# Six norms of a one-core block kernel: the sum of squares over the first three quarters moves from TensorE to VectorE

## The chip, the cores and the metric

The kernel runs on one core of one Trainium2 chip, in one launch. Five engines work from their own instruction streams and meet at semaphores: TensorE (PE, with its weight loads as PEld), VectorE (DVE), ScalarE (ACT), GpSimd (POOL, here only an issuer of DMAs) and SyncE (SP, also an issuer of DMAs). The metric is the device time of one launch in microseconds (us), as the median of several runs.

## The reference

A 256-token sequence of width 1024 in float32 passes one first block (Fourier mixing and a bidirectional gated delta rule, then a gated convolutional feed-forward net) and two hybrid layers (retention, gated linear recurrence and forgetting attention, merged, then an MLP). What matters here is that each of these six sublayers ends in a root-mean-square norm of its output before the residual addition:

```
def rms_norm(x, g):
    xf = x.astype(jnp.float32)
    y = xf * lax.rsqrt(jnp.mean(xf * xf, axis=-1, keepdims=True) + EPS)
    return (y * g.astype(jnp.float32)).astype(x.dtype)
...
    x = x + gt_m * rms_norm(merged @ w_out, g_post_mix)
    h = rms_norm(x, g_pre_mlp) * (1.0 + sc_f) + sh_f
    f = jnp.square(jax.nn.relu(h @ w1)) @ w2
    return x + gt_f * rms_norm(f, g_post_mlp)
```

The mean runs over the 1024 features of each token.

## The kernel before

**Layout.** Activations lie feature-major: 128 features on the partitions, eight feature blocks, 256 tokens along the free axis. A mean over features is therefore a sum over eight blocks and over the 128 partitions. TensorE does both at once: a 128x128 matrix `omean`, filled with 1/1024, is multiplied with each block of squares, and the eight products accumulate in PSUM bank 7, where every partition then holds the mean.

**The stream of chunks.** All weights come in 233 chunks of 1 MB, in the order of their use, into four slots `raw`, loaded by SP as soon as the chunk four places earlier is done. Each chunk is split in two parts for a three-product scheme: ScalarE writes `w_hi` (L1108), VectorE writes `w_lo` = raw - w_hi (L1651), into two slots each. TensorE then runs 48 products a chunk (16 weight tiles, three products each, L397 to L399), after a wait on `lo_ready`, and counts `chunk_done`. ScalarE may start on chunk n + 2 when chunk n is done. Queues are in program order on every engine; the order is written out by hand.

**The six norms.** They stand behind the output projection of the first block (`N_OUT1`, four chunks), its down-projection (`N_DOWN`, eleven chunks), and in each of two layers behind the output projection (`L_WOUT`, four chunks) and the second half of the MLP's down-projection (eight chunks, `deep_chunk`). Their outputs stay in four PSUM banks. When a bank (a quarter of the features) is complete, ScalarE squares it into SBUF (`square`, L1149, 128x512) and counts `norm_sq`. TensorE runs `norm_part` (L497 to L503) for that quarter: two products of plain float32, 128x256. For quarter q it stands one output bank behind: in the output projections the parts of quarters 0, 1 and 2 follow the chunks 1, 2 and 3, and in the two kinds of down-projection they follow the first product group of the next bank. The part of quarter 3 stands at the end. The last product counts `norm_ms`; ScalarE takes the root (`root`, L1154), VectorE the reciprocal (L1698), and the residual follows. Behind the norm, TensorE's queue goes on with products of a conditioning projection (`ada_mm`, L517), whose weights POOL loads when the buffers' last products are done.

The other seven norms (`norm`, L505) take their squares from SBUF, all four parts in a row, and are not touched.

Of the kernel before, what the change touches and what calls it, by code (L numbers as in the profile page):

```python
# [19 lines left out]
T = 256  # L20
# [70 lines left out]
def build_program(nc, io, layers=LAYERS):  # L91
# [6 lines left out]
    with ctx:  # L98
# [294 lines left out]
        def _(pe):  # L393
# [103 lines left out]
            def norm_part(k, sq, q):  # L497
# [4 lines left out]
                if q == 3:  # L502
                    last.then_inc(S("norm_ms"), 1)  # L503

            def norm(k, sq):  # L505
                for q in range(4):
                    norm_part(k, sq, q)
# [59 lines left out]
            for c in range(4):  # L567
                n = N_KV + c
                begin(n, n)
                bank = KV_BANK[c]  # L570
                feat_chunk(n % 2, bank + 1, 1)
                if c == 0:
                    pe.wait_ge(S("sw_wide"), 1)
                    pe.wait_ge(S("mod_lo"), 16)
                    small_mm(xc, 0)
                    small_mm(norm_h1, T).then_inc(S("ab_rows_mm"), 1)
                if c == 1:
                    pe.wait_ge(S("ab_rows"), 1)
                    small_tr(ab_rows, 4, 16).then_inc(S("ab_mm"), 1)
                feat_chunk(n % 2, bank, 0).then_inc(S("chunk_done"), 1)  # L580
# [286 lines left out]
            for c in range(4):  # L867
                begin(N_OUT1 + c, None)
                (turned_chunk if c == 0 else feat_chunk)((N_OUT1 + c) % 2, c, 1).then_inc(S("chunk_done"), 1)
                if c > 0:  # L870
                    norm_part(2, norm_sq1, c - 1)
            norm_part(2, norm_sq1, 3)
            ada_mm(14)
# [20 lines left out]
            for at_, (o, k, n, b) in enumerate(down):  # L894
                first_of_chunk, last_of_chunk = at_ % 16 == 0, at_ % 16 == 15
                if at_ == 34:
                    ada_tr(2)
                if first_of_chunk:
                    pe.wait_ge(S("lo_ready"), n + 1)
                if at_ == 0:  # L900
                    pe.wait_ge(S("evicted"), J_UP + 19)
                if o == 2 and k == 0:
                    pe.wait_ge(S("evicted"), J_DOWN)
                if o == 0 and k >= 16:
                    pe.wait_ge(S("mid_ready"), k + 1)
                last = mm3(ps[:, 2 + o // 2, o % 2 * T:o % 2 * T + T], w_hi[:, n % 2, b * P:(b + 1) * P], w_lo[:, n % 2, b * P:(b + 1) * P],
                           mid_hi1[:, k, :], mid_lo1[:, k, :], k == 0 and o % 2 == 0, k == FB - 1, shared=True)
                if last_of_chunk:
                    last.then_inc(S("chunk_done"), 1)
                elif o % 2 == 1 and k == FB - 1:  # L910
                    last.then_inc(S("down_done"), 1)
                if o % 2 == 0 and o >= 2 and k == FB - 1:
                    norm_part(4, sq_down, o // 2 - 1)
            norm_part(4, sq_down, 3)
            pe.wait_ge(S("ada_out"), 3)
# [3 lines left out]
            for L in range(layers):  # L919
# [129 lines left out]
                for c in range(4):  # L1049
                    n, j = n0 + L_WOUT + c, j0 + JL(L_WOUT) + c  # L1050
                    begin(n, j if c < 2 else None)
                    if c == 0:
                        out_chunk(n % 2, c, 0, 4 * L + 1).then_inc(S("chunk_done"), 1)
                    else:
                        feat_chunk(n % 2, c, 0).then_inc(S("chunk_done"), 1)
                        norm_part(ns + 1, a6, c - 1)
                norm_part(ns + 1, a6, 3)
                ada_mm(22 if L == 0 else 30)
# [6 lines left out]
                for hf in range(2):  # L1065
# [13 lines left out]
                    for c in range(8):  # L1079
                        begin(n + 8 + c, None)  # L1080
                        deep_chunk((n + 8 + c) % 2, c, hf, ready=all_ready if c == 0 else None).then_inc(S("chunk_done"), 1)
                        if hf == 1 and c % 2 == 0 and c >= 2:
                            norm_part(ns + 3, a6, c // 2 - 1)
                norm_part(ns + 3, a6, 3)
                if L == 0:
# [7 lines left out]
        def _(act):  # L1093
# [129 lines left out]
            for c in range(4):  # L1223
                n = N_KV + c
                prep(n + 2, (n + 2) % RAW, n % 2)
                if c == 0:
                    act.wait_ge(S("ab_rows_mm"), 1)
                    act_(ab_rows[:, :], ps[:, 7, :], ACT.Copy).then_inc(S("ab_rows"), 1)
                if c == 2:
# [412 lines left out]
        def _(dve):  # L1642
# [52 lines left out]
            def root_done(k):  # L1695
# [3 lines left out]
                dve.wait_ge(S("norm_rstd"), k + 1)  # L1699

            def pipe(m, pre, lo):

# [126 lines left out]
            def decay_part():  # L1829

                dve.wait_ge(S("ab_act"), 1)
                order(ts(sm[:, 2, :], sm[:, 2, :], 0.5, 0.5, ALU.mult, ALU.add))
# [194 lines left out]
            order(tt(gs[:, 0, :], mod[:, 16:24], V("g_post_mix", KT), ALU.mult))  # L2027
            job(N_OUT1, 3)
            dve.wait_ge(S("ada_out"), 1)
# [96 lines left out]

            job(N_DOWN, 9)
            layer_vectors(0)
# [3 lines left out]
            for L in range(layers):  # L2132
# [248 lines left out]
                for c in range(4):  # L2381
# [6 lines left out]
                    if c == 3:  # L2388
                        wout_lo(3)
                        prep(n + 2, (n + 2) % RAW, n % 2)  # L2390
                job(n0 + L_WOUT, 3)
                residual(ns + 1, 2 + 2 * L, 0, a5, gs[:, 0, :])
                prep(n0 + L_MLP + 1, (n0 + L_MLP + 1) % RAW, (n0 + L_MLP + 1) % 2)
                modulate(ns + 2, 4 + 2 * L, x, a5, gs[:, 1, :], mod[:, 24:32], act_hi[1], act_lo[1])
                for hf in range(2):
# [18 lines left out]
                    if hf == 1:  # L2414
                        mods_out()
                    job(n + 8, 8 if hf == 0 else 6)
                if L + 1 < layers:
# [144 lines left out]
```

## Time and profile before

| | us |
|---|---|
| median of 3 runs | 1755.04 (1750.12 to 1759.26) |
| the profiled execution | 1759.32 |
| its span, first to last instruction | 1757.5 |
| PE busy | 1664.9 (95%) |
| DVE busy | 1099.0 (63%) |
| ACT busy | 815.0 (46%) |

The span is 1.8 us shorter than the execution's own time. Busy times are unions over an engine's instructions; matmuls overlap each other in the pipeline, so that a matmul row's duration (280 ns) is longer than its distance to the next (114 to 118 ns). A product of plain float32 shows in the trace as two matmul instructions, so a part of a norm, two products, is a row of x4.

### The profile page before, as it was taken

What the parts mean: (1) busy time and instruction counts of PE and PEld (TensorE: products, weight loads), DVE (VectorE), ACT (ScalarE), POOL (GpSimd) and SP (SyncE); (2) the same over time, 40 slices, a digit from 0 to 9 for tenths busy, and PEclk for the clock granted to TensorE, in tenths of its full rate; (3) what the DMA queues carried; (4) which work ended last, traced back from release to release, by engine and by line L of the source; (5) the groups of instructions that cost most, each with busy time, mean ns of one, the idle gap of its engine ahead of it and who ended that gap; (6) DMA issues with size and microseconds to landing.
All of it is one profiled execution on the core that took longest, in us unless ns stands there. A gap on an engine that the chain in (4) does not pass through costs nothing.

```text
span 1757.5 us, 34379 instructions
## 1 busy us (share of the span) xinstructions
PE 1664.9 (95%) x15242; PEld 1586.6 (90%) x15242; DVE 1099.0 (63%) x1382; ACT 815.0 (46%) x1057; POOL 34.0 (2%) x68
## 2 busy tenths in 40 slices
PE   5997999999998999999998999989999999989997
PEld 4996888799996999999997999979999999979996
DVE  4576744689946455678866545455546878565463
ACT  3346324433434436458544434445454675444352
POOL 0001000000000000000001000000000000000000
PEclk8999999999999999999999999999999999999998
DMA  9336344744556446445559655555454555725551
GB/s 395 147 125 259 147 164 168 270 168 167 174 185 250 147 161 197 147 167 175 184 192 350 223 181 183 189 193 183 154 173 159 176 179 186 278 99 192 192 191 72
DMA packets 45529, 331.40 MB, mean 189 GB/s; under 512 B 5072, under 2 KB 5072, under 8 KB 5456
## 3 DMA queue, kind: packets, MB, share of 16 engines
q1 hardware_dynamic: 36032, 260.73, 42.9%
q0 software_dynamic: 9216, 67.11, 9.7%
q8 instruction: 113, 1.85, 0.4%
q10 hardware_dynamic: 144, 1.51, 0.2%
q14 instruction: 24, 0.20, 0.0%
HBM read 326.18 MB, written 1.05 MB: 186 GB/s over the span
## 4 chain that ended last, share of the span: by engine, by line
PE 80%; DVE 7%; ACT 5%; DMA 5%; issue 1%; SPq 1%; POOL 0%; ACTq 0%; DVEq 0%; POOLq 0%
PE ps L397 21%; PE ps L399 21%; PE ps L398 21%; PE ps L450 4%; DVE w_lo L1651 3%; ACT w_hi L1108 2%; PE ps L517 2%; DMA raw<-stream 2%; PE ps L501 2%; DMA ada_alt<-ada 1%; PE ps L674 1%; PE ps L685 1%; DMA ada_raw<-ada 1%; DMA ada_f<-ada 1%; PE ps L1002 1%
## 5 line engine op out<-in xcount | busy, mean ns | idle before, releaser
L397 PE MATMUL ps<-act_hi,w_hi 128*128 128x256 f32 x2672 | 757.6, 284 | 17.3 <-DVE act_lo L1720 4.6
L1651 DVE TENSOR_TENSOR w_lo<-raw,w_hi 128x2048 fp32r<-128x2048 f32 x207 | 474.4, 2292 | 467.9 <-ACT w_hi L1108 467.5
L398 PE MATMUL ps<-act_lo,w_hi 128*128 128x256 f32 x2672 | 747.9, 280 | 0.0
L399 PE MATMUL ps<-act_hi,w_lo 128*128 128x256 f32 x2672 | 747.8, 280 | 0.0
L1108 ACT ACTIVATE w_hi<-raw 128x2048 fp32r<-128x2048 f32 (+1 forms) x229 | 421.7, 1842 | 525.0 <-PE ps L399 506.1
L397 PEld LDWEIGHTS ps<-act_hi,w_hi 128*128 128x128 f32 x2672 | 507.3, 190 | 24.3 <-issue 13.3
L398 PEld LDWEIGHTS ps<-act_lo,w_hi 128*128 128x128 f32 x2672 | 506.8, 190 | 0.8
L399 PEld LDWEIGHTS ps<-act_hi,w_lo 128*128 128x128 f32 x2672 | 506.7, 190 | 0.0
L397 PE MATMUL ps<-mlp_hi,w_hi 128*128 128x256 f32 x512 | 143.9, 281 | 0.1
L398 PE MATMUL ps<-mlp_lo,w_hi 128*128 128x256 f32 x512 | 142.5, 278 | 0.0
L399 PE MATMUL ps<-mlp_hi,w_lo 128*128 128x256 f32 x512 | 142.5, 278 | 0.0
L398 PEld LDWEIGHTS ps<-mlp_lo,w_hi 128*128 128x128 f32 x512 | 96.8, 189 | 0.2
L397 PEld LDWEIGHTS ps<-mlp_hi,w_hi 128*128 128x128 f32 x512 | 96.3, 188 | 0.5 <-DVE w_lo L1659 0.3
L399 PEld LDWEIGHTS ps<-mlp_hi,w_lo 128*128 128x128 f32 x512 | 96.3, 188 | 0.0
L2076 DVE SCALAR_TENSOR_TENSOR gacc<-gpad,vectors,gacc 128x256 f32<-128x256 f32 x176 | 84.5, 480 | 15.6 <-ACT gacc L1379 10.3
L450 PE MATMUL ps<-h_up,raw 128*128 128x256 f32 x352 | 81.2, 381 | 0.7
L450 PEld LDWEIGHTS ps<-h_up,raw 128*128 128x128 f32 x352 | 64.7, 190 | 11.3 <-ACT h_up L1369 3.1
L397 PE MATMUL ps<-w_hi,act_hi 128*128 128x256 f32 x256 | 72.5, 283 | 0.0
L399 PE MATMUL ps<-w_hi,act_lo 128*128 128x256 f32 x256 | 71.6, 280 | 0.0
L398 PE MATMUL ps<-w_lo,act_hi 128*128 128x256 f32 x256 | 71.4, 279 | 0.0
L397 PE MATMUL ps<-mid_hi,w_hi 128*128 128x256 f32 x176 | 50.7, 288 | 3.7 <-DVE w_lo L1651 2.6
L1612 ACT ACTIVATE mlp_hi<-rsq 128x512 fp32r<-128x512 f32 x32 | 20.2, 632 | 72.6 <-DVE rsq L2403 72.6
(420 smaller groups left out, 2008.1 us busy)
## 6 DMA issues: line engine op xcount, KB each, us to landing
raw<-stream SPq DMA_DIRECT2D x233, 1024.0 KB, 4.9
ada_raw<-ada POOLq DMA_DIRECT2D x46, 1024.0 KB, 6.6
ada_alt<-ada POOLq DMA_DIRECT2D x12, 1024.0 KB, 12.1
ada_f<-ada POOLq DMA_DIRECT2D x6, 1024.0 KB, 8.7
ada_f<-ada SPq DMA_DIRECT2D x4, 1024.0 KB, 13.9
ada_a<-ada SPq DMA_DIRECT2D x3, 1024.0 KB, 20.0
s<-s SPq DMA_DIRECT2D x4, 512.0 KB, 10.1
consts_stage<-consts_a SPq DMA_DIRECT2D x1, 1728.0 KB, 32.7
```

Of the source, the lines that this page charges most:

```text
L397: mm(out, ah, bh, start=first, stop=False, skip_group_check=shared)
L398: mm(out, ah, bl, start=False, stop=False, skip_group_check=shared)
L399: return mm(out, al, bh, start=False, stop=last, skip_group_check=shared)
L450: mm(ps[:, bank, 0:T], raw[:, slot, k * P:(k + 1) * P], h_up[:, k, :], start=k == 0, stop=k == KT - 1)
L501: last = mm(ps[:, 7, 0:T], omean, sq[:, b, :], start=b == 0, stop=b == KT - 1)
L517: last = mm(ps[strip:strip + 32, bank, c * T:(c + 1) * T], cs_wide[:, k, 32 - 3 * j:64 - 3 * j], ada_home(i, c)[:, k * T:(k + 1) * T], sta ...
L674: last = mm(ps[r:r + 64, INV_BANK[q], j * 64:(j + 1) * 64], B01[d][r:r + 64, t0 + j // 4, j % 4, r:r + 64], Tm[r:r + 64, q, j, :], start=T ...
L685: last = mm(ps[r:r + 64, INV_BANK[q], j * 32:(j + 1) * 32], Uc[r:r + 64, q, j, :], half(X[r:r + 64, q, j, :], d, 1 << lvl), start=True, st ...
L1108: act_(w_hi[:, s2, o:CH], raw[:, s4, o:CH], ACT.Copy).then_inc(S("hi_ready"), 1)
L1612: act_(mlp_hi[:, bass.ds((i + c) * 2, 2), :], rsq[:, s, :].rearrange("p (b t) -> p b t", b=2), ACT.Copy)\
L1651: tt(w_lo[:, s2, :], raw[:, s4, :], w_hi[:, s2, :].bitcast(f32), ALU.subtract).then_inc(S("lo_ready"), 1)
L2076: ins = stt(acc, src, w, acc, ALU.mult, ALU.add)
```

## The change

The products between the chunks are gone from the six norms. VectorE adds quarter 1 of the squares onto quarter 0 (128x512), later quarter 2 onto the result, and then folds the two blocks of the result into one (128x256), counting a new semaphore `norm_pre`. TensorE runs three products behind the last chunk: the folded block once `norm_pre` has come, and the two blocks of quarter 3 once their squares have come. A second edit frees one semaphore for this: the ScalarE copy that counted `ab_rows` now counts `ab_act`, and VectorE's later wait on `ab_act` asks for 2 in place of 1.

```diff
+            def norm_folded(i, k, sq):
+
+                pe.wait_ge(S("norm_pre"), i + 1)
+                mm(ps[:, 7, 0:T], omean, sq[:, 0, :], start=True, stop=False)
+                pe.wait_ge(S("norm_sq"), 4 * k + 4)
+                mm(ps[:, 7, 0:T], omean, sq[:, 6, :], start=False, stop=False)
+                mm(ps[:, 7, 0:T], omean, sq[:, 7, :], start=False, stop=True).then_inc(S("norm_ms"), 1)
...
-                    pe.wait_ge(S("ab_rows"), 1)
+                    pe.wait_ge(S("ab_act"), 1)
...
                 (turned_chunk if c == 0 else feat_chunk)((N_OUT1 + c) % 2, c, 1).then_inc(S("chunk_done"), 1)
-                if c > 0:
-                    norm_part(2, norm_sq1, c - 1)
-            norm_part(2, norm_sq1, 3)
+            norm_folded(0, 2, norm_sq1)
...
-                if o % 2 == 0 and o >= 2 and k == FB - 1:
-                    norm_part(4, sq_down, o // 2 - 1)
-            norm_part(4, sq_down, 3)
+            norm_folded(1, 4, sq_down)
...
                         feat_chunk(n % 2, c, 0).then_inc(S("chunk_done"), 1)
-                        norm_part(ns + 1, a6, c - 1)
-                norm_part(ns + 1, a6, 3)
+                norm_folded(2 + 2 * L, ns + 1, a6)
...
-                        if hf == 1 and c % 2 == 0 and c >= 2:
-                            norm_part(ns + 3, a6, c // 2 - 1)
-                norm_part(ns + 3, a6, 3)
+                norm_folded(3 + 2 * L, ns + 3, a6)
...
+            def square_sum(k, sq, q):
+
+                dve.wait_ge(S("norm_sq"), 4 * k + q + 1)
+                order(tt(sq[:, 0:2, :], sq[:, 0:2, :], sq[:, 2 * q:2 * q + 2, :], ALU.add))
+                if q == 2:
+                    tt(sq[:, 0, :], sq[:, 0, :], sq[:, 1, :], ALU.add).then_inc(S("norm_pre"), 1)
...
-                dve.wait_ge(S("ab_act"), 1)
+                dve.wait_ge(S("ab_act"), 2)
...
-            job(N_OUT1, 3)
+            job(N_OUT1, 2)
+            square_sum(2, norm_sq1, 1)
+            job(N_OUT1 + 2, 1)
+            square_sum(2, norm_sq1, 2)
...
-            job(N_DOWN, 9)
+            job(N_DOWN, 7)
+            square_sum(4, sq_down, 1)
+            job(N_DOWN + 7, 2)
+            square_sum(4, sq_down, 2)
...
-                job(n0 + L_WOUT, 3)
+                job(n0 + L_WOUT, 2)
+                square_sum(ns + 1, a6, 1)
+                job(n0 + L_WOUT + 2, 1)
+                square_sum(ns + 1, a6, 2)
...
-                    job(n + 8, 8 if hf == 0 else 6)
+                    if hf == 0:
+                        job(n + 8, 8)
+                    else:
+                        job(n + 8, 4)
+                        square_sum(ns + 3, a6, 1)
+                        job(n + 12, 2)
+                        square_sum(ns + 3, a6, 2)
```

(`order(...)` marks an instruction and has VectorE wait for its end; `job` on VectorE writes the `w_lo` of so many chunks.)

How the queues change is seen at three places. The first is TensorE's queue before, at the boundary of chunks 1 and 2 of the first block's output projection (act_hi_54, act_lo_56 are the split activations, norm_sq_116 the squares, consts_common holds `omean`):

```order
L397 MATMUL ps<-act_hi_54,w_hi 128x256
L398 MATMUL ps<-act_lo_56,w_hi 128x256
L399 MATMUL ps<-act_hi_54,w_lo 128x256
L501 MATMUL ps<-norm_sq_116,consts_common 128x256 [waits norm_sq]
L501 MATMUL ps<-norm_sq_116,consts_common 128x256
L397 MATMUL ps<-act_hi_54,w_hi 128x256 [waits lo_ready]
L398 MATMUL ps<-act_lo_56,w_hi 128x256
```

Now the chunks follow each other without a break there. The second place is the end of that projection, in TensorE's queue with the change (L508 takes the folded block, L510 and L511 the fourth quarter, L525 is `ada_mm`):

```order
L397 MATMUL ps<-act_hi_54,w_hi 128x256
L398 MATMUL ps<-act_lo_56,w_hi 128x256
L399 MATMUL ps<-act_hi_54,w_lo 128x256
L508 MATMUL ps<-norm_sq_116,consts_common 128x256 [waits norm_pre]
L510 MATMUL ps<-norm_sq_116,consts_common 128x256 [waits norm_sq]
L511 MATMUL ps<-norm_sq_116,consts_common 128x256
L525 MATMUL ps<-ada_raw,silu_c_wide 32x256 [waits ada_loaded0]
```

Before, four L501 stood in the place of L508 to L511, with one wait ahead of each pair. The third place is VectorE's queue with the change, in the same projection (L1652 is the `w_lo` split, L1705 and L1707 are the new additions, L1699 the reciprocal of the root):

```order
L1652 TENSOR_TENSOR w_lo<-raw,w_hi 128x2048 [waits hi_ready]
L1705 TENSOR_TENSOR norm_sq_116<-norm_sq_116 128x512 [waits norm_sq]
L1652 TENSOR_TENSOR w_lo<-raw,w_hi 128x2048 [waits hi_ready,dve_order]
L1705 TENSOR_TENSOR norm_sq_116<-norm_sq_116 128x512 [waits norm_sq]
L1707 TENSOR_TENSOR norm_sq_116<-norm_sq_116 128x256 [waits dve_order]
L2041 TENSOR_TENSOR mod<-mod_raw,vectors 128x24 [waits ada_out]
L2043 SCALAR_TENSOR_TENSOR gain_scale<-mod,vectors 128x8 [waits mods_done]
L2044 TENSOR_TENSOR gain_scale<-mod,vectors 128x8 [waits dve_order]
L1699 RECIPROCAL rstd<-std 128x256 [waits norm_std,dve_order]
```

Before, the splits stood there back to back. One addition now stands between the last two splits, and the other two stand behind the last.

## Rows read from the trace of the kernel before

**Rows 1.** The page: busy times of the engines; shares of the chain by line.

```profile
PE 1664.9 (95%) x15242; PEld 1586.6 (90%) x15242; DVE 1099.0 (63%) x1382; ACT 815.0 (46%) x1057; POOL 34.0 (2%) x68
PE ps L397 21%; PE ps L399 21%; PE ps L398 21%; PE ps L450 4%; DVE w_lo L1651 3%; ACT w_hi L1108 2%; PE ps L517 2%; DMA raw<-stream 2%; PE ps L501 2%; DMA ada_alt<-ada 1%; PE ps L674 1%; PE ps L685 1%; DMA ada_raw<-ada 1%; DMA ada_f<-ada 1%; PE ps L1002 1%
```

**Rows 2.** The chain in order of time, layer 0's output projection: start, us, what.

```profile
947.11 1.82 PE ps L501 x8
948.93 3.63 PE ps L517 x64
952.85 11.37 DMA ada_alt<-ada
```

**Rows 3.** Timeline of PE, first block's output projection and last MLP: start, us, instruction, xcount.

```profile
308.19 0.28 PE L399 MATMUL ps<-act_hi,w_lo 128*128 128x256 f32 x1
308.31 1.02 PE L501 MATMUL ps<-norm_sq,consts_common 128*128 128x256 f32 x4
...
309.29 0.28 PE L398 MATMUL ps<-act_lo,w_hi 128*128 128x256 f32 x1
...
314.70 0.28 PE L399 MATMUL ps<-act_hi,w_lo 128*128 128x256 f32 x1
...
315.80 0.28 PE L398 MATMUL ps<-act_lo,w_hi 128*128 128x256 f32 x1
...
321.04 0.28 PE L399 MATMUL ps<-act_hi,w_lo 128*128 128x256 f32 x1
...
1736.81 0.28 PE L399 MATMUL ps<-mlp_hi,w_lo 128*128 128x256 f32 x1
1736.92 1.02 PE L501 MATMUL ps<-s,consts_common 128*128 128x256 f32 x4
...
1737.90 0.28 PE L398 MATMUL ps<-mlp_lo,w_hi 128*128 128x256 f32 x1
```

**Rows 4.** Stretches: us; PE, PEld, DVE, ACT, POOL busy (x); granted clock; DMA; GB/s.

```profile
504.00:508.00 4.00, 4.00 (x38) 4.00 (x37) 2.29 (x1) 1.94 (x2) 0.00 (x0) 1.00 0.79 262
928.00:932.00 4.00, 4.00 (x36) 4.00 (x36) 1.61 (x2) 2.40 (x2) 0.00 (x0) 1.00 1.01 426
936.00:940.00 4.00, 4.00 (x38) 4.00 (x37) 2.29 (x1) 0.96 (x2) 0.00 (x0) 1.00 1.01 426
1124.00:1128.00 4.00, 4.00 (x36) 4.00 (x35) 0.11 (x1) 1.61 (x1) 0.00 (x0) 1.00 0.23 39
1134.00:1138.00 4.00, 4.00 (x38) 4.00 (x37) 2.28 (x1) 0.00 (x0) 0.00 (x0) 1.00 0.50 209
1704.00:1708.00 4.00, 4.00 (x38) 4.00 (x37) 2.29 (x1) 0.28 (x1) 0.00 (x0) 1.00 0.57 233
```

**Rows 5.** Timeline of DVE, end of the first block's output projection.

```profile
317.03 2.29 DVE L1651 TENSOR_TENSOR w_lo<-raw,w_hi 128x2048 fp32r<-128x2048 f32 x1 [4.22 <-ACT w_hi L1108]
319.24 0.18 DVE L2030 TENSOR_TENSOR mod<-mod_raw,vectors 128x24 f32<-128x24 f32 x1
```

**Rows 6.** DVE additions of like form: all of L2356 (min/median/max ns), one L2038.

```profile
L2356 DVE TENSOR_TENSOR s<-s,s x8: 691/693/694, 910.6 to 1520.3; 128x512 f32<-128x512 f32 x8
...
338.10 0.42 DVE L2038 TENSOR_TENSOR act_lo<-h_up,act_hi 128x256 fp32r<-128x256 f32 x1 [0.23 <-ACT act_hi L1371]
```

**Rows 7.** Timeline of ACT, three squares and two roots, first block and layer 0's MLP.

```profile
316.90 0.58 ACT L1149 ACTIVATE norm_sq<-ps 128x512 f32<-128x512 f32 x1
...
321.35 0.60 ACT L1149 ACTIVATE norm_sq<-ps 128x512 f32<-128x512 f32 x1 [3.78 <-PE ps L399]
323.17 0.47 ACT L1154 ACTIVATE std<-ps,eps 128x256 f32<-128x256 f32 x1 [1.22 <-PE ps L501]
...
1150.07 0.60 ACT L1149 ACTIVATE s<-ps 128x512 f32<-128x512 f32 x1 [4.07 <-PE ps L399]
1151.89 0.47 ACT L1154 ACTIVATE std<-ps,eps 128x256 f32<-128x256 f32 x1 [1.22 <-PE ps L501]
```

**Rows 8.** Timeline of DVE behind layer 0's MLP: the next layer's first split.

```profile
1146.11 2.29 DVE L1651 TENSOR_TENSOR w_lo<-raw,w_hi 128x2048 fp32r<-128x2048 f32 x1 [2.19 <-ACT w_hi L1108]
```

More of the change, by code:

```diff
@@ L1227, in _ @@
                     act.wait_ge(S("ab_rows_mm"), 1)
-                    act_(ab_rows[:, :], ps[:, 7, :], ACT.Copy).then_inc(S("ab_rows"), 1)
+                    act_(ab_rows[:, :], ps[:, 7, :], ACT.Copy).then_inc(S("ab_act"), 1)
                 if c == 2:
```

## The prediction

> **What bounds the kernel now.** I read the page's busy times first, then the chain of work that ended last, then the timelines around the six norms. PE is busy for 1664.9 of 1757.5 us and its product lines make up most of the chain; the norm products (L501) alone hold 2% of the chain [rows 1]. So time that leaves PE's queue leaves the launch, unless another engine or a transfer ends the same stretch just as late. At a chunk boundary with a norm part, the timeline shows what the part costs: the last chunk product before it starts at 308.19 and the second one behind it at 309.29 [rows 3]. PE is not idle in between and waits for nothing.
>
> **Products between the chunks: removed.** From 308.19 to 309.29 are 1.10 us, of which two steps of 0.118 would pass anyway: the part costs 0.86 us. The last of its kind, in layer 1's MLP, costs the same: 1737.90 - 1736.81 - 2 x 0.114 = 0.86 us [rows 3]. I count how many such parts stand ahead of a last chunk: in the three output projections quarters 0 and 1, in the down-projection and the two MLPs quarters 0, 1 and 2, so 3 x 2 + 3 x 3 = 15. That is 15 x 0.86 = 12.9 us, all in PE's order and so on the chain.
>
> The Trainium skill ("TensorE: Matmul & The Clock Gate", section "Back-to-back issue gap") gives an isolated matmul of N columns a gap of N / 2.4 + 2.5 ns at the full clock, 109 ns for 256. By it the four matmul instructions of a part would cost an estimated 0.44 us and the sum would be 6.5 us, not a gain that the measurement could tell. The trace disagrees for plain float32 (0.86 us a part [rows 3]); only the products of the split scheme come near the page's figure, at 114 to 118 ns. The measured part is used.
>
> **Products at the end: two fewer or one more, at no cost or gain.** In the output projections quarter 2 stood behind the last chunk too. The last square starts at 321.35, the root at 323.17: 1.82 us. Behind layer 0's MLP, where only quarter 3 stood at the end, square to root is 1151.89 - 1150.07 = 1.82 us as well [rows 7]. So the two extra products were already hidden under the square, and the chain there is square, two products, root, which the change keeps. The new product of the folded block (half of 0.86, 0.43 us) goes under the same square: that starts 0.20 us after the last chunk's products (321.04 + 0.11 [rows 3], 321.35) and lasts 0.60 [rows 7], so there is 0.80 us of cover.
>
> **The additions on VectorE.** Per norm two of 128x512 and one of 128x256. An addition of that kind in place took 0.69 us, one of 128x256 0.42 us [rows 6]: 1.80 us a norm, 10.8 us of VectorE over the launch, which is busy 63% [rows 1]. Three places could feel them.
> - *The next split.* The first addition stands behind a split and ahead of the next. In the tightest stage the split starts at 317.03, 2.21 us after the end of its chunk (314.70 + 0.12 [rows 3]), and the next instruction starts 2.21 later [rows 5]; an addition then ends about 5.1 us after the chunk, and the next split starts 5.4 + 2.2 = 7.6 us after it. Slack 2.5 us. The split itself ends 2.21 + 2.29 = 4.5 us after the chunk, and the chunk that needs it starts at 5.4 us at the earliest (48 products of 0.114). So PE, without the parts, still finds its weights 0.9 us early. Were this cover gone, each of 15 boundaries would keep a part of its 0.86 us.
> - *The folded block.* In the output projections the last two additions come behind the split of 317.03: 2.21 + 2.21 + 0.69 + 0.42 = 5.5 us after the end of chunk 2, plus two hand-overs between engines or instructions, of at most 0.2 us each (the 0.20 us from the last product to the square): 5.5 to 5.9 us. The last chunk ends after 5.4 (fast) or 5.7 us (slow, below); the folded product has to start 0.80 - 0.43 = 0.37 us later to stay under the square, by 5.8 to 6.0 us. So it is in hand or at worst 0.1 us late, at three norms: 0 to 0.3 us, and I take 0, nearer to most of the range. In the other three norms a whole chunk lies between.
> - *What is queued behind them.* Behind the MLP the next layer's vectors and first split follow; that split waited 2.19 us for ScalarE [rows 8], more than the 1.1 us of two additions. Nobody else waits there.
>
> The wait of the first addition is for a square that ends at most 0.1 us behind the start of VectorE's split of the same chunk (316.90 + 0.58 against 317.03 + 2.29 in the same pattern [rows 5, 7]), so it blocks nothing. The semaphore edit moves no instruction: the same copy counts, the same readers wait. Cost nothing.
>
> **The pace of the chunk products: a loss.** At a granted clock of 1.00, PE issues the chunk products at one of two paces. Between the two parts of the first projection 46 steps take 314.70 - 309.29 = 5.41 us, 118 ns each; behind the second part 46 steps take 321.04 - 315.80 = 5.24 us, 114 ns each [rows 3]. The same two paces are in the stretches of 4 us with 36 and with 38 products, and it is not the transfers: 928 to 932 and 936 to 940 have the same DMA share [rows 4]. A pace holds until something interrupts the run of products. In the output projections and in layer 0's MLP, a norm part was what ended a slow pace; without parts I expect the slow one to hold to the stage's end. That hits 48 products in the first projection, 2 x 96 in the layers' (the stretches 928 and 936 are layer 0's), and 144 in layer 0's MLP (1124 and 1134): 384 x 4 ns = 1.5 us. The down-projection and layer 1's MLP run fast already (504, 1704 [rows 4]); what set that stays, so I take no loss there. Bounds: 0 if the pace rises by itself, and if these two are slow as well 528 + 384 products more, 3.6 us, so 5.1 us.
>
> **Sum.** 12.9 - 1.5 = 11.4 us saved. The profiled execution took 1759.3 us, so its like would take 1747.9. It stood 4.3 us above the median of the runs, 1755.04, from which I forecast 1743.6 us (-0.65%).
>
> **Rivals.**
> 1. *Transfers or the clock take part of it back.* Behind layer 0's output projection the chain goes from the norm over `ada_mm` into an 11.37 us transfer [rows 2]; the down-projection's and layer 0's MLP's norms end alike. If these transfers ended at a fixed time, three stages would lose their 2 + 3 + 3 parts, 8 x 0.86 = 6.9 us, and 6.0 - 1.5 = 4.5 us of gain would remain: 1750.5. Against it: they are issued when `ada_mm` has freed its buffers, so they begin earlier too. Chance 0.10.
> 2. *The pace falls further.* All six stages slow from start to end: 12.9 - 5.1 = 7.8 us saved, 1747.2, within 0.5%. For it: the paces changed just behind norm parts. Against: the fast stages entered so without one. Chance 0.13.
> 3. *The folded block is late, or the change does not take the parts' time with it.* VectorE's additions behind the split, or TensorE left waiting at boundaries for `lo_ready`. If two thirds of the parts' time turned into waiting, 4.3 - 1.5 = 2.8 us would remain: 1752. Against it the 0.9 us of slack above. Chance 0.04. The page's gap rule would end here too (6.5 - 1.5 = 5.0 us, 1750); the rows leave it a chance of 0.02.
> 4. *Slower.* The interrupted run decides the pace for what follows: a layer has 93 chunks of 48 products, and if 93 chunks that now run fast run slow, that is 4464 x 4 ns = 17.9 us, and 1755.0 - 12.9 + 17.9 = 1760. The change loses from 12.9 / 0.004 = 3225 products, 67 chunks, on. For it: the pace is set by small things, and runs of the kernel differ by 9 us. Against: between the norms and the chunks that follow stand other products and waits, which set the pace anew. Chance 0.05.
>
> **How the numbers follow.** The forecast has 0.66. 0.5% (8.8 us) is about what a measurement of this kernel can tell from no change; single runs before spread over 9 us, so I put some 3 us of spread on a difference of medians. The forecast's 11.4 us lie 2.6 us beyond the bound, so about 0.53 of its 0.66 come out faster by over 0.5% and 0.13 within. Of rival 2's 0.13 some 0.05 do, of rival 1's 0.10 some 0.02, of rival 3 and the page's rule none worth a number. Rival 4 is slower with all of its 0.05. Faster 0.60, within 0.5% 0.35, slower 0.05. The range: down, no loss of pace and one MLP stage of 1000 products moved to the fast pace, 12.9 + 4.0, with some 2 us of spread: 1736. Up, rivals 1 and 3: 1752.
>
> **What would show it.** In the changed kernel's trace: chunk products 0.114 to 0.118 us apart across the 15 boundaries, with no wait on VectorE; square to root still 1.82 us at all six ends; the new additions 0.69, 0.69 and 0.42 us, the folded product before the last square's end; 36 products in 4 us to the end of the output projections and of layer 0's MLP. The prediction is wrong if PE waits for `lo_ready` at the boundaries, if a root comes later than 1.9 us after the last square's start, if the transfers behind the norms keep their old times, or if stages away from the norms change their pace.

## The result, and the profile after

Timed together with the kernel before, the changed kernel took 1736.56 us (median of 4 runs, 1733.56 to 1738.21) against 1755.35 us. The ratio is 0.9907, 95% interval 0.9883 to 0.9931: 16.3 us less, between 12.1 and 20.5. The forecast was 1743.6 us and 11.4 us less, with a range of 1736 to 1752, so the time lies half a microsecond inside its low end. Two later comparisons of the same two kernels, told below as experiments, gave ratios of 0.9943 and 0.9931. Weighted by the widths of their intervals (a narrow one counts more) the three make 0.9925 (0.9910 to 0.9941), which is 13.1 us (10.4 to 15.8) of 1753. The first comparison stands at the high end of that, and part of the work below is telling 13 from 16.

The profiled execution took 1738.21 us. Its page, busy times of the engines and then the first part of the shares of the chain by line (line numbers have moved by one or more; the norm helpers are now L501 for whole norms and L508, L510 and L511 for folded ones):

```profile
PE 1648.1 (95%) x15182; PEld 1570.4 (90%) x15182; DVE 1108.8 (64%) x1400; ACT 813.8 (47%) x1057; POOL 34.0 (2%) x68
PE ps L397 19%; PE ps L399 19%; PE ps L398 19%; DVE w_lo L1652 5%; PE ps L450 4%; ACT w_hi L1109 4%; DMA raw<-stream 2%; PE ps L525 2%; DMA ada_alt<-ada 1%; PE ps L693 1%; PE ps L682 1%; DVE rsq L2420 1%; DMA ada_raw<-ada 1%; DVE rstd L1699 1%; PE ps L501 1%
```

Against [rows 1] PE is busy 16.8 us less, VectorE 9.8 us more, and the norm line L501 has gone from 2% to 1% of the chain. PE still bounds the kernel. In this trace the chain passes through VectorE and ScalarE more often, because it follows two waits of PE for a weight split (of 0.3 us each, in layer 0's MLP, not at a boundary that the change touched) back along those engines. That is not the change's mark: VectorE's share of the chain is 7% before, 12% here, 8% in the third trace of the changed kernel and 10% with the semaphore edit alone.

What the change took out shows in the timeline of PE at the end of the first block's output projection, with the columns of [rows 3]:

```profile
307.21 0.28 PE L399 MATMUL ps<-act_hi,w_lo 128*128 128x256 f32 x1
307.32 0.28 PE L397 MATMUL ps<-act_hi,w_hi 128*128 128x256 f32 x1
...
312.65 0.28 PE L399 MATMUL ps<-act_hi,w_lo 128*128 128x256 f32 x1
313.01 0.70 PE L508 MATMUL ps<-norm_sq,consts_common 128*128 128x256 f32 x2
313.61 0.70 PE L510 MATMUL ps<-norm_sq,consts_common 128*128 128x256 f32 x2
314.15 0.59 PE L511 MATMUL ps<-norm_sq,consts_common 128*128 128x256 f32 x2
314.67 0.42 PE L525 MATMUL ps<-ada_raw,silu_c_wide 128*32 128x256 f32 x4
```

The last product of one chunk starts at 307.21 and the first of the next 0.11 us later, where a part of 1.02 us stood before. The whole last chunk is 312.65 - 307.21 = 5.44 us, 48 steps of 0.113. In the three traces of the changed kernel no step from product to product across the 15 boundaries is longer than 0.119 us, so PE waits for no split there. The next two fences are VectorE and ScalarE in the same stretch:

```profile
304.10 2.29 DVE L1652 TENSOR_TENSOR w_lo<-raw,w_hi 128x2048 fp32r<-128x2048 f32 x1 [3.08 <-ACT w_hi L1109]
306.31 0.68 DVE L1705 TENSOR_TENSOR norm_sq<-norm_sq 128x512 f32<-128x512 f32 x1
309.61 2.29 DVE L1652 TENSOR_TENSOR w_lo<-raw,w_hi 128x2048 fp32r<-128x2048 f32 x1 [2.62 <-ACT w_hi L1109]
311.81 0.69 DVE L1705 TENSOR_TENSOR norm_sq<-norm_sq 128x512 f32<-128x512 f32 x1
312.53 0.42 DVE L1707 TENSOR_TENSOR norm_sq<-norm_sq 128x256 f32<-128x256 f32 x1
```

```profile
312.96 0.60 ACT L1150 ACTIVATE norm_sq<-ps 128x512 f32<-128x512 f32 x1 [2.89 <-PE ps L399]
314.78 0.47 ACT L1155 ACTIVATE std<-ps,eps 128x256 f32<-128x256 f32 x1 [1.22 <-PE ps L511]
...
1131.41 0.60 ACT L1150 ACTIVATE s<-ps 128x512 f32<-128x512 f32 x1 [3.18 <-PE ps L399]
1133.23 0.47 ACT L1155 ACTIVATE std<-ps,eps 128x256 f32<-128x256 f32 x1 [1.22 <-PE ps L511]
```

The additions take 0.69 (0.68) and 0.42 us, as [rows 6] promised, and the next split still idles 2.62 us for ScalarE behind them. Square to root is 314.78 - 312.96 = 1.82 us, as in [rows 7], and it is 1.82 at all six ends. From the view of the folded product's line (L508), for which engine and line TensorE waited, with the us in all and the number of times:

```profile
  DVE norm_sq L1707: 0.3, 1
  DVE s L1707: 0.3, 1
```

So two of six folded products waited for the fold, 0.3 us each, and still ended under the square. The transfer behind layer 0's output projection answers to [rows 2], in the chain in order of time:

```profile
938.28 3.63 PE ps L525 x64
942.20 11.00 DMA ada_alt<-ada
```

It started 942.20 - 936.50 = 5.70 us after the last square (936.50 from ScalarE's timeline); before, it was 952.85 - 947.15 = 5.70. The transfer moved with the norm. So did the one behind the down-projection, 5.70 us after its last square in both traces (555.34 - 549.64 and 543.17 - 537.47).

**The stages over several executions.** Single traces mislead here. In the first pair of traces the first projection's stage lost 9.6 us where 1.7 were due. So I took for each stage the span from the root of the whole norm ahead of it to the root of the folded norm that ends it, in three executions without the change (the profile before, the semaphore edit alone, and the kernel before a second time) and in three with it. The three values in us, with their mean in brackets:

```
stage (ends in a folded norm)  without the change           with it                      mean change  parts x 0.865
first output projection        301.7 294.0 293.8  (296.5)   292.1 296.1 296.2  (294.8)   -1.7         -1.7
down-projection                217.2 215.6 214.5  (215.7)   214.5 216.4 214.5  (215.2)   -0.6         -2.6
layer 0, output projection     387.6 391.3 387.9  (388.9)   387.9 386.7 386.9  (387.2)   -1.8         -1.7
layer 0, MLP                   193.0 187.9 191.0  (190.7)   185.0 185.1 191.0  (187.0)   -3.6         -2.6
layer 1, output projection     384.1 387.1 383.7  (385.0)   383.4 383.4 383.0  (383.2)   -1.7         -1.7
layer 1, MLP                   188.6 188.5 187.3  (188.1)   185.9 185.9 188.9  (186.9)   -1.2         -2.6
sum                                                                                      -10.6        -13.0
```

The spread inside a row is larger than the change of a row. With three executions each, the sum of -10.6 us can't be told from -13.0 or from the forecast's -11.4, and by itself not from -16 either. The whole spans differ by 9.8 us on average (1750.6 and 1740.7).

The granted clock doesn't explain the gain either. The mean clock of the spans was 0.983, 0.986 and 0.990 without the change and 0.985, 0.986 and 0.983 with it. That makes an estimated 60, 49 and 35 us at half the clock without it and 52, 49 and 59 with it, so not less.

### The profile page after: what moved, and what is told of

The parts are those of the page before. It is cut to its first block, busy times and chain, and to the rows that moved or that the text cites. A ratio compares the mean times of both kernels' runs of the same rounds, so it can differ in the third digit from the quotient of the medians.

```text
span 1736.4 us, 34270 instructions
## 1 busy us (share of the span) xinstructions
PE 1648.1 (95%) x15182; PEld 1570.4 (90%) x15182; DVE 1108.8 (64%) x1400; ACT 813.8 (47%) x1057; POOL 34.0 (2%) x68
## 4 chain that ended last, share of the span: by engine, by line
PE 74%; DVE 12%; ACT 8%; DMA 4%; issue 2%; SPq 1%; POOL 0%; ACTq 0%; DVEq 0%; POOLq 0%
PE ps L397 19%; PE ps L399 19%; PE ps L398 19%; DVE w_lo L1652 5%; PE ps L450 4%; ACT w_hi L1109 4%; DMA raw<-stream 2%; PE ps L525 2%; DMA ada_alt<-ada 1%; PE ps L693 1%; PE ps L682 1%; DVE rsq L2420 1%; DMA ada_raw<-ada 1%; DVE rstd L1699 1%; PE ps L501 1%
## 5 line engine op out<-in xcount | busy, mean ns | idle before, releaser
L1652 DVE TENSOR_TENSOR w_lo<-raw,w_hi 128x2048 fp32r<-128x2048 f32 x207 | 474.4, 2292 | 448.9 <-ACT w_hi L1109 448.3
L2087 DVE SCALAR_TENSOR_TENSOR gacc<-gpad,vectors,gacc 128x256 f32<-128x256 f32 x176 | 84.7, 482 | 15.7 <-ACT gacc L1380 10.4
```

What stands on the lines that cost most here:

```text
L1652: tt(w_lo[:, s2, :], raw[:, s4, :], w_hi[:, s2, :].bitcast(f32), ALU.subtract).then_inc(S("lo_ready"), 1)
L2087: ins = stt(acc, src, w, acc, ALU.mult, ALU.add)
```

## The experiments

Each kernel was timed in turn with the kernel before on the same chip; ratios are against that, with their 95% intervals.

**The semaphore edit alone.**

```diff
-                    pe.wait_ge(S("ab_rows"), 1)
+                    pe.wait_ge(S("ab_act"), 1)
```

> The kernel before with only the second edit (the copy counts ab_act, VectorE's later wait asks for 2). Theory A (the gain is the 15 parts' 13.0 us of TensorE time, and what was measured beyond it is the chance of pace and granted clock in single executions): no change, 1755 us within 0.5%; square to root 1.82 us at all six norms, 15 boundaries with 0.86 us each; the half-clock stretches and the slow runs of chunk products lie elsewhere than in the profile of before. Theory B (the edit in the first block's early code is what sped the first 300 us, 9.6 us less up to the first root of the six where 1.7 us were due): 1749 us or less, and the root behind the first output projection near 315 us in place of 323 us.

Measured: 1751.54 us, ratio 0.9989 (0.9968 to 1.0011). No difference beyond the noise, though theory B's 1749 us (a ratio of 0.9975) lies inside the interval. In its profile the first projection took 294.0 us and the end of layer 0's MLP ran fast, with all parts in place. The short first projection is what theory B foretold, so this run alone doesn't refute it. The kernel before without the rename does: its second trace, below, had 293.8 us. So those two stages can come out short without the change and without the rename, and this kernel serves as a second "before".

**The fold at the output projections only, and at the other three norms only.** Each takes the change's lines for three norms and leaves the parts in the other three. The first takes out 6 of the 15 parts, the second 9 (edits against the kernel before, one line each):

```diff
-                norm_part(ns + 1, a6, 3)
+                norm_folded(1 + L, ns + 1, a6)
...
```

> The change only in the three output projections; the down-projection and the two MLPs keep their parts. Theory A: 6 x 0.865 = 5.2 us less than before, 1750 us, with square to root 1.82 us everywhere. Theory C (the gain comes with the longer unbroken runs, whose pace rises): more than 5.2 us, 8 to 9, since these three had slow runs.

```diff
-                norm_part(ns + 3, a6, 3)
+                norm_folded(1 + L, ns + 3, a6)
...
```

> The change only in the down-projection and the two MLPs. Theory A: 9 x 0.865 = 7.8 us less, 1747.5 us. Theory C: layer 0's MLP stage falls by about 8 us as in the changed kernel and the sum is 13 us, 1742 us.

Measured: 1744.97 us, ratio 0.9963 (0.9941 to 0.9986), 6.5 us less where 5.2 were due; and 1742.32 us, ratio 0.9939 (0.9917 to 0.9962), 10.7 us less where 7.8 were due. Each half gains by itself, about in the proportion of its parts, and together they make 17.2 us, about as much as the first comparison. That excludes a gain that sits in one stage or needs all six. The times don't decide against theory C, whose 8 to 9 and 13 us lie inside the intervals (2.5 to 10.3 and 6.7 to 14.6); the traces do. In the first of these kernels both layers' output projections were slow to their ends (the table of slow products below), in the second layer 0's MLP took 190.8 us, not 8 less than 193.0. The longer unbroken runs didn't rise in pace.

**The first three quarters not summed at all.** The mean square lacks them, there are no parts and no additions:

```diff
-                if c > 0:
-                    norm_part(2, norm_sq1, c - 1)
-            norm_part(2, norm_sq1, 3)
+            norm_part(2, norm_sq1, 3, only=True)
```

> The kernel before with the semaphore edit, and without the norm parts of quarters 0 to 2 of the six norms: no products and no additions for them, so the six norms sum over the last quarter alone. Theory A: the same time as the changed kernel within 0.5%, 13 us less than before, since VectorE's additions and the folded product cost nothing. A rival in which VectorE's additions cost time: this one is faster than the changed kernel by more than 3 us.

Measured: 1734.19 us, ratio 0.9891 (0.9857 to 0.9924), 19.1 us less where 13 were due (13.3 to 25.1). Taken with the pooled ratio of the changed kernel, the fold and its product cost 0.0034 of 1753 us, 6.0 us, with an interval of -0.5 to 12.4. The interval reaches zero and this comparison doesn't settle it. Against the two halves of the change, timed in the same comparison (17.2 us together), only 1.9 us remain. The traces don't show where the fold would cost: square to root is 1.82 us in both kernels, and PE waits at none of the 15 boundaries.

**The parts twice.** Here those quarters count twice in the mean.

```diff
-                    norm_part(2, norm_sq1, c - 1)
+                    norm_part(2, norm_sq1, c - 1, times=2)
```

> The kernel before (with the semaphore edit) in which each of the 15 parts between chunks is issued twice, so that these quarters count twice in the mean. Theory A (a part costs its own 0.865 us, four instructions in PE's order): +13.0 us against the kernel before, about 1766. Rival B (it is the interruption of the run of chunk products that costs, not the part's own time; a boundary is interrupted either way): 0 to +3 us. Rival D (PE has spare time at the boundaries because it waits for weights or transfers anyway): 0.

Measured: 1767.53 us, ratio 1.0088 (1.0055 to 1.0121): 15.4 us more, between 9.6 and 21.2. The expectation overlooked that the same line also doubles quarter 2 of the three output projections, which stands behind the last chunk; there square to root grew to 2.59 us. Corrected, the sum is 13.0 + 3 x 0.77 = 15.3 us. ScalarE's timeline of the first projection, with the waits in brackets, gives the price of a doubled part:

```profile
306.67 1.91 ACT L1110 ACTIVATE w_hi<-raw 128x2048 fp32r<-128x2048 f32 x1 [3.04 <-PE ps L399]
...
314.05 1.91 ACT L1110 ACTIVATE w_hi<-raw 128x2048 fp32r<-128x2048 f32 x1 [4.98 <-PE ps L399]
...
321.38 0.60 ACT L1151 ACTIVATE norm_sq<-ps 128x512 f32<-128x512 f32 x1 [4.83 <-PE ps L399]
323.97 0.47 ACT L1156 ACTIVATE std<-ps,eps 128x256 f32<-128x256 f32 x1 [1.99 <-PE ps L502]
```

Chunk end to chunk end is 314.05 - 306.67 = 7.38 us; without 48 steps of 0.118 (5.65) 1.73 remain, 0.865 for each part. A part costs its own time on PE's path. Rivals B and D fall.

**All parts behind the last chunk.** The same products, none between chunks, no additions:

```diff
-                if c > 0:
-                    norm_part(2, norm_sq1, c - 1)
-            norm_part(2, norm_sq1, 3)
+            norm(2, norm_sq1)
```

> The kernel before (with the semaphore edit) with all four parts of a norm behind the last chunk: the same products, none between chunks, no addition on VectorE. Theory A (products cost their time wherever PE has nothing else hidden beside them): 15 x 0.865 = 13.0 us go from between the chunks, and behind the last chunk three parts of 0.865 = 2.6 us have only the 0.80 us of the last square to lie beside, so that each of six roots comes 1.8 us later than square to root 1.82: about 3.6 us from square to root, and 13.0 - 6 x 1.8 = 2 us faster than the kernel before. Rival B (runs of chunk products without an interruption are what gains): about as much as the change, 10 us or more.

Measured: 1746.98 us, ratio 0.9973 (0.9951 to 0.9996), 4.7 us less, between 0.7 and 8.6. PE and then ScalarE at the end of layer 0's MLP:

```profile
1131.62 0.28 PE L399 MATMUL ps<-mlp_hi,w_lo 128*128 128x256 f32 x1
1131.73 3.61 PE L501 MATMUL ps<-s,consts_common 128*128 128x256 f32 x16
1135.28 0.42 PE L517 MATMUL ps<-ada_raw,silu_c_wide 128*32 128x256 f32 x4
```

```profile
1131.93 0.60 ACT L1142 ACTIVATE s<-ps 128x512 f32<-128x512 f32 x1 [3.18 <-PE ps L399]
1135.38 0.47 ACT L1147 ACTIVATE std<-ps,eps 128x256 f32<-128x256 f32 x1 [2.86 <-PE ps L501]
```

The sixteen instructions run back to back, and the root comes 3.45 us after the square's start at all six ends, 1.63 later than before: 13.0 - 6 x 1.63 = 3.2 us, inside the interval. Rival B's 10 us lie outside it. So taking the interruptions away is not what gains. The products must leave PE, or lie beside something else.

**Four more additions ahead of the fold.**

```diff
                 if q == 2:
+                    for _ in range(4):
+                        order(tt(sq[:, 2:4, :], sq[:, 2:4, :], sq[:, 4:6, :], ALU.add))
                     tt(sq[:, 0, :], sq[:, 0, :], sq[:, 1, :], ALU.add).then_inc(S("norm_pre"), 1)
```

> The changed kernel with four more additions of 128x512 (into blocks that nobody reads again) ahead of the last fold of each norm: 4 x 0.69 = 2.76 us more of VectorE per norm, 16.6 us in all. Theory A (VectorE's additions are hidden as long as the folded product starts under the last square; only the three output projections, where the last two additions come behind the split of the chunk before last, have less cover than this): about +2.5 us at each of these three, 7.5 us in all against the changed kernel, nothing at the other three, so 1744 to 1746. Rival C (the additions cost everywhere, by VectorE's queue or by taking turns at the memory): +12 us and more. Rival E (the folded product has far more cover): 0.

Measured: 1748.47 us, ratio 0.9989 (0.9969 to 1.001). Against the changed kernel of the same comparison that is 0.9989 / 0.9943 = 1.0046, 8.1 us more (2.1 to 14.0). The roots say where: square to root is 4.72, 5.92 and 4.34 us at the three output projections, and 1.82 at the other three, 9.5 us in all. Theory A holds in its places, and its 7.5 us in size within the noise. Rival C's 12 us lie inside the interval of the time; it falls by the three norms that pay nothing. PE in layer 0's output projection, then two stretches there, two at the end of the first block's output projection and one at layer 1's, with the granted clock (third column from the end):

```profile
937.22 0.28 PE L399 MATMUL ps<-act_hi,w_lo 128*128 128x256 f32 x1
940.49 1.22 PE L508 MATMUL ps<-s,consts_common 128*128 128x256 f32 x2 [3.00 <-DVE s L1709]
941.50 1.06 PE L510 MATMUL ps<-s,consts_common 128*128 128x256 f32 x2
942.35 1.06 PE L511 MATMUL ps<-s,consts_common 128*128 128x256 f32 x2
```

```profile
940.00:942.00 2.00, 1.51 (x4) 1.25 (x5) 0.42 (x1) 0.00 (x0) 0.00 (x0) 0.61 0.84 340
942.00:944.00 2.00, 2.00 (x12) 0.96 (x14) 0.04 (x1) 0.55 (x2) 0.00 (x0) 0.54 0.04 16
314.00:316.00 2.00, 1.49 (x6) 1.06 (x6) 0.85 (x4) 0.00 (x0) 0.00 (x0) 0.95 0.86 356
316.00:318.00 2.00, 2.00 (x21) 0.93 (x24) 1.16 (x1) 1.73 (x2) 0.00 (x0) 0.50 0.00 0
1532.00:1534.00 2.00, 1.55 (x10) 1.12 (x14) 0.39 (x1) 0.00 (x0) 0.00 (x0) 1.00 0.86 365
```

PE waits 3.00 us for the fold. At this end the granted clock also falls to about half (1.2 of 2.4 GHz) behind the wait, and a product of two instructions takes 0.85 to 1.0 us instead of 0.43 to 0.54; that is most of the difference between 5.92 and the other two. At the first block's output projection, behind a wait of 3.00 us as well, it falls only around the last of the three products. At layer 1's, behind 2.78 us, it stays at 1.00 through all three.

**The same two kernels again.** The changed kernel twice more and the kernel before once more, with no edit.

> The changed kernel once more, nothing else. Theory A (the parts' 15 x 0.865 = 13.0 us leave PE's path; what goes beyond it comes from the pace of the chunk products and from half-clock stretches that each execution draws anew): 13 to 16 us below the kernel before, and the trace of this execution has the same 5.44 us boundaries, but stages whose chunk products run at the other pace (113.5 or 118 ns) than in the first trace, and half-clock stretches at other times. Rival B (the change itself sets the paces and so gains the rest): the same stages fast and slow as in the first trace of the changed kernel.

> The kernel before against itself, with a second trace. Theory A (the pace of a stage belongs to the execution, not to the parts): ratio 1 within its interval; layer 0's MLP, 193.0 us at 118 ns a product in the first trace, may come out at either pace, 187.5 us if fast; the first projection's stage anywhere from 291 to 302 us. Rival B (the parts hold the slow pace): layer 0's MLP again 193 us, the first projection again 301.7.

> The changed kernel a third time, to narrow the two measurements so far (16.3 and 10.0 us below the kernel before). Theory A: 13 us below, within 11 and 15. Rival B (the change also gains by the paces): 16 us or more. The forecast's own sum (13 less 1.5 of pace): 11.4 us.

Measured: the changed kernel 1741.72 us, ratio 0.9943 (0.9916 to 0.9969), and 1744.27 us, ratio 0.9931 (0.9901 to 0.9962); the kernel before against itself 1751.94 us, ratio 0.9999 (0.9979 to 1.0019). So the gain is 10.0 (5.4 to 14.7) and 12.1 us (6.7 to 17.4) in these. The 10.0 lie below the 13 to 16 that the second execution was expected to show, and their interval takes in the low end. A gain of 16 us or more, the rival's, lies just outside the pooled interval. The other rival of the second execution, that the change sets the paces, falls by its trace: the down-projection and layer 0's output projection were slow to their ends, where the first trace had them fast. Layer 0's MLP with its parts took 187.9 and 191.0 us where the first trace had 193.0, and without them it took 185.0, 185.1 and 191.0: executions differ by more than its parts are worth.

The two paces are plain when two executions of one kernel are laid side by side. ScalarE's timeline at layer 0's output projection, the two last weight casts, each released by the end of a chunk; first the first execution of the changed kernel, then the second:

```profile
925.68 1.92 ACT L1109 ACTIVATE w_hi<-raw 128x2048 fp32r<-128x2048 f32 x1 [3.10 <-PE ps L399]
...
931.12 1.92 ACT L1109 ACTIVATE w_hi<-raw 128x2048 fp32r<-128x2048 f32 x1 [3.04 <-PE ps L399]
```

```profile
928.45 1.92 ACT L1109 ACTIVATE w_hi<-raw 128x2048 fp32r<-128x2048 f32 x1 [3.26 <-PE ps L399]
...
934.10 1.92 ACT L1109 ACTIVATE w_hi<-raw 128x2048 fp32r<-128x2048 f32 x1 [3.26 <-PE ps L399]
```

A chunk of 48 products takes 5.44 us in the one and 5.65 in the other, with the same code. Here is how many of the chunk products between the first removed part's place and the stage's end were slow (the step from one product's start to the next over 0.116 us), counted from the timelines of PE:

```
                            out 1   down      out L0  MLP L0    out L1  MLP L1    all
before, first trace         50/93   6/326     5/94    100/235   5/93    3/236     169 of 1077
semaphore edit alone        3/94    6/326     5/93    3/236     2/94    3/236     22 of 1079
before, second trace        4/94    6/326     4/93    6/236     5/93    6/236     31 of 1078
parts twice                 94/94   326/326   48/94   236/236   94/94   236/236   1034 of 1080
changed, first trace        0/95    0/330     0/95    0/240     95/95   0/240     95 of 1095
changed, second trace       0/95    330/330   95/95   0/240     95/95   0/240     520 of 1095
changed, third trace        95/95   0/330     0/95    0/240     95/95   0/240     190 of 1095
fold at down and MLPs only  4/94    0/330     5/94    240/240   5/94    0/240     254 of 1092
fold at output proj. only   0/95    3/324     95/95   6/234     95/95   8/234     207 of 1077
parts left out              0/95    0/330     0/95    0/240     94/95   0/240     94 of 1095
parts behind last chunk     0/95    0/330     95/95   0/240     95/95   0/240     190 of 1095
changed, four additions     0/95    0/330     0/95    0/240     95/95   0/240     95 of 1095
```

With single parts the products behind a part run fast almost always. Without parts a stage's end is all fast or all slow, as it came in. With double parts nearly everything behind them is slow. Counted part by part, by the pace of the products just ahead of a part and of those behind it: of the 60 single parts in five traces 46 stood behind products at the fast pace, and all kept that pace; 14 stood behind products at the slow pace, and 12 of these ended it. Of the 15 double parts 5 stood behind products at the fast pace, and all ended it; 10 stood behind products at the slow pace, and 9 kept it.

## Why the prediction was right

**Products between the chunks.** Right. 15 x 0.86 = 12.9 us was the term that carried the sum; the doubled parts gave 0.865 us each, and the kernel with all parts behind the last chunk lost most of its gain again where the products came back onto the path. PE waits at none of the 15 boundaries, as forecast. The rule of the Trainium skill weighed there ("TensorE: Matmul & The Clock Gate", section "Back-to-back issue gap") would have made it an estimated 6.5 us; that is outside the pooled interval of 10.4 to 15.8.

**Products at the end.** Right: 1.82 us at all six ends in all three traces. The condition is shown too: with 2.6 us of products behind the last chunk the cover of 0.80 us is gone.

**The additions.** Right, and right about how near the edge they are. In the first trace the fold of layer 0's output projection ended at 936.07 + 0.42 = 936.49, the folded product started at 936.55, and the product behind it could not start before the square's end at 936.50 + 0.60 = 937.10. That leaves 937.10 - 936.55 - 0.43 = 0.12 us; the first block's output projection has the same (313.56 - 313.01 - 0.43). Wherever such a stage ended at the slow pace, as layer 1's did, 0.33 us were left: the slow chunk gives VectorE more time. The four extra additions, 2.76 us, came through whole at the three output projections and not at all at the others, where a whole chunk of cover was counted. One reading in the prediction is wrong without harm: the square that the first addition waits for ends 0.45 us behind the start of the split (317.48 against 317.03), not 0.1. The addition stands behind the end of that split, so nothing hangs on it.

**The pace: right in kind, half right in place.** I forecast 384 products more at the slow pace, 1.5 us. The three traces with the change have 95, 520 and 190 slow products in these stretches, 268 on average, the three without it 169, 22 and 31, 74 on average: 194 products x 4.5 ns = 0.9 us. That a part mostly ends a slow pace (12 of 14), and that a slow pace entered without parts holds to the stage's end, both show in the table and the counts below it. Layer 1's output projection was slow to its end every time, as forecast, the other two in one trace of three each. But layer 0's MLP, where I put 144 of the 384 products, was fast at its end in all three traces of the changed kernel, against the sign that was named for it (its pace in the first trace before was a draw of that execution), and the down-projection, for which I took no loss, was slow in one. The step "the down-projection and layer 1's MLP run fast already; what set that stays" failed once in three for the down-projection: I read a single trace as the kernel's habit.

**The sum.** 12.9 - 1.5 = 11.4 us against 13.1 (10.4 to 15.8) measured, and 13.0 - 0.9 = 12.1 with the terms as the traces now give them. The first comparison's 1736.56 us stood 7.0 below the forecast, and that it still fell inside the range, by half a microsecond, was luck. Of the 7.0 us, 13.1 - 11.4 = 1.7 are the pooled gain beyond the forecast; the rest did not repeat in the two later comparisons, which had the changed kernel at 1741.72 and 1744.27.

**The rivals.** Transfers that keep their old times: no, the one behind layer 0's output projection and the one behind the down-projection moved with their norms to the hundredth; layer 0's MLP's is no longer on the chain. The pace falls further: the second trace went half of that way (520 of 1095) and its comparison gave the smallest gain, 10.0 us, though one execution's pace proves nothing about a median. The folded block late: it waited twice, hidden. Slower by the pace of what follows: no comparison shows it. Over the whole launch about 5070, 5440 and 6880 products were slow with the change and about 5680, 5080 and 5240 without it, some 460 more on average with the change. That is 2.1 us against it, on three draws each with a larger spread. Whether a loss of that size is real stays open. The last sign of being wrong, that stages away from the norms change their pace, could not decide anything: they do so from one execution of the same program to the next.

## What to carry to other kernels

Where one engine bounds the kernel without gaps, work that is moved from it to an engine with slack gains the time that it held in the first engine's order, if its result is in hand before the next wait of that engine would end anyway. Moving the work to another place on the same engine gains only what finds cover there (here 4.7 us, between 0.7 and 8.6). Read the cover where it is thinnest, not on average: here 2.76 us of extra work was free at three norms and cost 2.5 to 4.1 us at the other three. And when executions of one program differ by more than the change, take several traces of both before explaining a stage.

## What the runs showed of the hardware beyond that

- The same products, at a granted clock of 1.00, run at 0.113 or 0.118 us a step, and which of the two holds can differ between executions of the same program. Over a launch with some 10,600 such steps between about 4170 (parts left out) and 7060 (fold at down and MLPs only) were slow in the profiled executions: 2890 x 4.5 ns = 13 us of difference, as much as the whole change. Of one and the same program, the changed kernel, it was 5070 to 6880.
- The four instructions of one part leave PE in the fast pace nearly always (58 of 60 parts); eight leave it in the slow one nearly always (14 of 15). Why was not tried.
- Waits of PE of 3.00, 3.00 and 2.78 us were followed by three different courses of the granted clock: a fall to half at once, with the six product instructions behind the wait taking about twice as long; a fall to 0.50 about 1.3 us after the wait's end; and none through the three products.
